# Two decoder blocks in one kernel: the forgetting term as a three-part bfloat16 product, and the turns of the probabilities at the end of a part

## The reference

```python
def forgetting_attention(q, k, v, log_f):       # 8 heads of 64
    c = jnp.cumsum(log_f, axis=1).transpose(0, 2, 1)
    ...
        s = jnp.einsum('bqhd,bkhd->bhqk', qb, k).astype(jnp.float32) * scale
        s = s + cq[..., None] - c[:, :, None, :]
        s = jnp.where((key_pos[None, :] <= qpos[:, None])[None, None], s, -jnp.inf)
        p = jax.nn.softmax(s, axis=-1).astype(v.dtype)
        return jnp.einsum('bhqk,bkhd->bqhd', p, v)
```

## Time and profile before

| | us |
|---|---|
| median of 3 runs (1918.96 to 1920.2) | 1919.72 |
| time of the profiled execution | 1919.35 |
| its span in the profile | 1917.2 |
| PE busy | 1901.4 |
| DVE busy | 1334.5 |
| ACT busy | 973.6 |

### The profile page before, as it was taken

The page is one execution under the profiler, slowest core; times in us unless marked ns, Lnnn a source line. Parts: engine busy times, 40 slices in busy tenths (PEclk is TensorE's granted clock), DMA queues, the critical chain, the costliest instruction groups (busy, mean ns, idle before and its releaser), DMA issues.

```text
span 1917.2 us, 26196 instructions
## 1 busy us (share of the span) xinstructions
PE 1901.4 (99%) x10969; PEld 1646.5 (86%) x10972; DVE 1334.5 (70%) x1461; ACT 973.6 (51%) x1227; POOL 151.7 (8%) x158
## 2 busy tenths in 40 slices
PE   9999999999999999999999999999999999999998
PEld 7888878888888888798888888888888888888887
DVE  7886677787678766868776554569865655569763
ACT  5444565544444445655444565445444665455442
POOL 0000422100000005211000110000000110000000
PEclk9999999999999999999999999999999999999999
DMA  7555533454555555324545443454555343445552
GB/s 285 208 183 185 194 111 111 154 198 170 184 198 194 175 199 183 121 95 161 191 179 186 151 175 132 175 177 166 196 182 185 130 163 138 166 176 182 181 181 105
DMA packets 47493, 327.31 MB, mean 171 GB/s; under 512 B 5520, under 2 KB 5520, under 8 KB 11536
## 3 DMA queue, kind: packets, MB, share of 16 engines
q1 hardware_dynamic: 46512, 323.25, 47.1%
q10 hardware_dynamic: 864, 2.39, 0.3%
HBM read 324.57 MB, written 1.05 MB: 170 GB/s over the span
## 4 chain that ended last, share of the span: by engine, by line
PE 95%; DVE 2%; ACT 1%; issue 1%; DMA 0%; POOL 0%; DVEq 0%; POOLq 0%; SPq 0%; ACTq 0%
PE ps L539 34%; PE ps L541 17%; PE ps L527 10%; PE ps L529 9%; PE ps L528 9%; PE ps L533 2%; PE ps L830 2%; PE ps L785 1%; PE ps L787 1%; PE ps L786 1%; PE ps L796 1%; PE ps L534 1%; PE ps L819 1%; PE ps L706 1%; PE ps L800 1%
## 5 line engine op out<-in xcount | busy, mean ns | idle before, releaser
L332 ACT CAST w_hi<-raw 128x2048 fp32r<-128x2048 f32 (+3 forms) x314 | 580.2, 1849 | 580.9 <-PE ps L541 351.8
L339 DVE TENSOR_TENSOR w_lo<-raw,w_hi 128x2048 fp32r<-128x2048 f32 (+3 forms) x314 | 699.1, 2228 | 246.2 <-ACT w_hi L332 243.4
L539 PE MATMUL ps<-x_hl,w_hi 128*128 128x512 f32 x1968 | 494.3, 393 | 0.0
L539 PEld LDWEIGHTS ps<-x_hl,w_hi 128*128 128x128 f32 x1968 | 353.8, 189 | 63.6
L541 PEld LDWEIGHTS ps<-x_hl,w_lo 128*128 128x128 f32 x1968 | 268.4, 190 | 19.3
L541 PE MATMUL ps<-x_hl,w_lo 128*128 128x256 f32 x1968 | 274.3, 282 | 0.0
L527 PE MATMUL ps<-w_hi,x_hl 128*128 128x512 f32 (+3 forms) x672 | 261.9, 390 | 0.0
L529 PE MATMUL ps<-w_hi,x_hl 128*128 128x512 f32 (+3 forms) x672 | 254.3, 378 | 0.0
L528 PE MATMUL ps<-w_lo,x_hl 128*128 128x512 f32 (+3 forms) x672 | 253.5, 377 | 0.0
L1789 DVE TENSOR_REDUCE ffn_tmp<-ps 128x512 f32<-128x1024 f32 x132 | 161.2, 1222 | 103.4 <-PE ps L541 102.6
L539 PE MATMUL ps<-hid_hl,w_hi 128*128 128x512 f32 x836 | 212.9, 394 | 0.0
(11 more groups left out here) (286 smaller groups left out, 2216.3 us busy)
## 6 DMA issues: line engine op xcount, KB each, us to landing
raw<-in_parts SPq DMA_DIRECT2D x278, 1024.0 KB, 4.8
raw<-in_parts SPq DMA_DIRECT2D x20, 768.0 KB, 4.1
raw<-in_parts SPq DMA_DIRECT2D x4, 928.0 KB, 4.5
raw<-in_parts SPq DMA_DIRECT2D x4, 864.0 KB, 4.7
raw<-in_parts SPq DMA_DIRECT2D x6, 512.0 KB, 3.7
raw<-in_parts SPq DMA_DIRECT2D x4, 576.0 KB, 3.9
const<-in_const ACTq DMA_DIRECT2D x1, 1098.0 KB, 5.2
h<-in_x_t SPq DMA_DIRECT2D x1, 1024.0 KB, 8.0
```

What stands on the lines that cost most here:

```text
L332: nc.scalar.copy(w_hi[:, i % RING, 0:n_of(i)], raw[:, i % RING, 0:n_of(i)]).then_inc(high_ready, 1)
L339: nc.vector.tensor_tensor(w_lo[:, s, 0:n], raw[:, s, 0:n], w_hi[:, s, 0:n].bitcast(F32), ALU.subtract).then_inc(low_ready, 1)
L539: nc.tensor.matmul(ps[:, bank, :], w_h(c), hl(c).rearrange("p x n -> p (x n)"), start=start and c == 0, stop=False, skip_group_check=True)
```

## The change

1. **Forgetting term.** `log_f` now holds the negated log gates three times, in columns 0 to 7, 32 to 39 and 64 to 71. The cumulated sums therefore stand three times in the bank. ACT copies the bank once to the bfloat16 tile `forget`; DVE subtracts this from the bank, writes the rest's bfloat16 over rows 32 to 63, and what is then left over rows 64 to 127. The products of line 800 now take `forget` and one column of the constant `head_rows`, which has ones in the three rows of the head, repeated to 128 columns; both are bfloat16. The part with c of the query is gone. `head_rows` is made once, in the first stage.
2. **Turns.** In both mixers PE's `batch_turn` of parts 10 to 14 and 16 to 19 moves from between the halves to the start of `after_part`, ahead of the scores. With it go two turns of q and k blocks (`qk_turn(7)` and `qk_turn(8)`).
3. **Copies.** In `mixer1` DVE's copy of a turned batch moves behind the `top_rounds` of its part, and in part 14 behind the gating. In part 12 it stands behind two rounds and ahead of `scale_heads`. In `mixer2` DVE's and ACT's lists are as before.

```diff
@@ constants
-    q_mul, q_add, k_mul, k_add = np.zeros((P, 8)), np.zeros((P, 8)), np.zeros((P, 1)), np.zeros((P, 1))
...
+    c["head_rows"] = (s % 32 == np.arange(8)[None, :]) * (s < 96) * 1.0
@@ batches1
-                        aug=[(q_aug[h0 + i][:, qt * P:(qt + 1) * P], k_aug[:, 0:nk]) for i in range(4)] if gate else None,
+                        aug=[(head_rows[:, h0 + i:h0 + i + 1].to_broadcast([P, P]), forget[:, 0:nk]) for i in range(4)] if gate else None,
@@ PE, mixer1
+                def after_part(m):
                     if m == 10:
                         pe.wait_ge(S["relu_ready"], 8)
                         turn_p(0)
...
-                def after_part(m):
...
-                        pe.wait_ge(S["aug_ready"], 9)
+                        pe.wait_ge(S["aug_ready"], 2)
                         qk_turn(6)
...
+                        pe.wait_ge(S["aug_ready"], 3)
                         scores(0)
@@ ACT, mixer1
-                    nc.scalar.activation(k_aug, cum, ACT.Identity, scale=cst("k_mul"), bias=cst("k_add")).then_inc(S["aug_ready"], 1)
-                    for hd in range(6):
-                        nc.scalar.activation(q_aug[hd], cum, ACT.Identity, scale=cst("q_mul")[:, hd:hd + 1],
-                                             bias=cst("q_add")[:, hd:hd + 1]).then_inc(S["aug_ready"], 1)
+                    nc.scalar.copy(forget[:, :], cum).then_inc(S["aug_ready"], 1)
@@ DVE, mixer1
+                def forget_terms():
+
+                    dve.wait_ge(S["aug_ready"], 1)
+                    nc.vector.tensor_tensor(forget_rest, ps[:, 1, 0:SEQ], forget[:, :], ALU.subtract).then_inc(S["aug_ready"], 1)
+                    dve.wait_ge(S["aug_ready"], 2)
+                    nc.vector.tensor_copy(forget[32:64, :], forget_rest[32:64, :])
+                    step(nc.vector.tensor_copy(forget[64:128, :], forget_rest[64:128, :]))
+                    nc.vector.tensor_tensor(forget[64:128, :], forget_rest[64:128, :], forget[64:128, :],
+                                            ALU.subtract).then_inc(S["aug_ready"], 1)
...
-                    if m >= 10:
-                        turned_p(m - 10)
                     if m == 12:
                         top_rounds(2)
+                        turned_p(2)
...
                     top_rounds({10: 4, 11: 4, 13: 2}.get(m, 0))
+                    if m >= 10 and m != 12:
+                        turned_p(m - 10)
...
-                        for hd in range(6, 8):
-                            nc.vector.tensor_scalar(q_aug[hd], ps[:, 1, 0:SEQ], cst("q_mul")[:, hd:hd + 1], cst("q_add")[:, hd:hd + 1],
-                                                    ALU.mult, ALU.add).then_inc(S["aug_ready"], 1)
+                        forget_terms()
```

More of the change, by code:

```diff
@@ L240, in build @@
         later_bf = sb("later_bf", [P, P], BF16)
+        head_rows = sb("head_rows", [P, 8], BF16)
+        forget = sb("forget", [P, SEQ], BF16)
         stat = sb("stat", [P, 212])
@@ L400, in build @@
         rope_a, rope_b = region(17824, (576,)), region(17824 + 576, (576,))
-        q_aug = ([proj[:, x // 2, C_Q + SEQ * (x % 2):C_Q + SEQ * (x % 2) + SEQ] for x in range(4)] +
-                 [proj[:, x // 2, I_Q + SEQ * (x % 2):I_Q + SEQ * (x % 2) + SEQ] for x in range(1, 4)] + [rows[:, 0, 0:SEQ]])
-        k_aug = proj[:, 0, I_Q:I_Q + SEQ]
+        forget_rest = proj[:, 0, I_Q:I_Q + SEQ]
         relu_r = ffn_tmp[:, 0:1024].rearrange("p (a b c) -> p a b c", a=2, b=2)
@@ L1187, in _ @@
                 if s == 1:
-                    pe.wait_ge(setup_done, 2)
+                    pe.wait_ge(setup_done, 3)
                 if tag == "mix":
@@ L1257, in ffn @@
                         nc.scalar.copy(later_bf[:, :], cst("later")).then_inc(setup_done, 1)
+                        act.wait_ge(tables_in, 16)
+                        nc.scalar.copy(head_rows[:, :], cst("head_rows")).then_inc(setup_done, 1)
                     if s == LAST and p in (7, 10, 13, 16):
@@ L2031, in after_part @@
                         dve.wait_ge(S["ln_ready"], 2)
-                        step(nc.vector.scalar_tensor_tensor(log_f[:, :, 0:8], z_f, 0.0, z_abs, ALU.min, ALU.subtract))
-                        nc.vector.tensor_scalar(log_f[:, :, 32:40], log_f[:, :, 0:8], -1.0, None, ALU.mult).then_inc(S["logf_ready"], 1)
+                        step(nc.vector.scalar_tensor_tensor(z_ln, z_f, 0.0, z_abs, ALU.min, ALU.subtract))
+                        for x in range(3):
+                            f = nc.vector.tensor_scalar(log_f[:, :, 32 * x:32 * x + 8], z_ln, -1.0, None, ALU.mult)
+                        f.then_inc(S["logf_ready"], 1)
                     if m == 7:
@@ L2038, in after_part @@
                         add_index(3)
-                        dve.wait_ge(S["aug_ready"], 7)
-                        for hd in range(6, 8):
-                            nc.vector.tensor_scalar(q_aug[hd], ps[:, 1, 0:SEQ], cst("q_mul")[:, hd:hd + 1], cst("q_add")[:, hd:hd + 1],
-                                                    ALU.mult, ALU.add).then_inc(S["aug_ready"], 1)
+                        forget_terms()
                     if m == 9:
```

## The result

| | before | with the change |
|---|---|---|
| median of 20 runs each, us | 1919.29 | 1922.57 |
| lowest and highest, us | 1918.85, 1920.23 | 1922.14, 1923.28 |
| profiled execution, us | 1919.35 | 1923.28 |
| its span, us | 1917.2 | 1921.2 |
| PE, DVE, ACT busy, us | 1901.4, 1334.5, 973.6 | 1899.3, 1338.1, 967.1 |

The changed kernel takes 1.0017 times as long as the kernel before, with a 95% interval of 1.001 to 1.0023. It is slower by 3.3 us, and the prediction had 1915.8 with a range of 1912.5 to 1919.5. The forecast missed by 6.8 us, and the time lies outside its range.

What follows compares the result with a forecast made beforehand. PE, busy 1901.4 of 1917.2 us, was taken as the bound. The first mixer's -5.4 and the second's +1.4 gave -4.0 us; with 0.37 to the median and 0.1 for signals, 1915.8 us, range 1912.5 to 1919.5.

Steps and rivals of the forecast that it cites:

- rival (B): Part 10, first mixer: the clock falls in PE's new wait; 1918.8 or 1926.9 us; chance short 0.14, long 0.05.
- short case: Low clock lasts as long as the wait in part 10: 1.5 us a layer, 1918.8 us; chance 0.14.
- long case: All of part 11 runs at the low clock: 5.56 us a layer, 1926.9 us; chance 0.05.
- the term: Forgetting products, first mixer: four at the mask's price, 0.77 us less for 128 keys, 1.39 less for 256.
- Rival (C): Forgetting products: the repeated column costs what float32 did; 3.1 us lost in all, 1918.9 us; chance 0.08.
- the wait of part 10: First mixer: PE stands still 3.1 us ahead of batch 0's values, for DVE's copy behind all six rounds.
- the 0.53 us of `qk_turn(6)`: Part 9, first mixer: the bank is free earlier, so this turn and what follows move 0.53 us earlier.
- The tie of part 11: First mixer: PE reaches the values at 280.1, with DVE's copy ready at 280.0.
- rival (D): A moved copy is later than the wait it removes; in part 12 too, 1916.8 us; chance with forecast 0.67.
- Part 13: First mixer: PE arrives at 297.9 and waits 1.8 us for the copy of batch 3; values start at 299.7.
- the second mixer: Openings save 0.3 us, a new wait in part 19 costs 1.0: 0.7 us more a layer, 1.4 in all.
- Rival (A): Copies come in time and PE keeps all: 6.2 us a layer in the first mixer, 1908.7 us; chance 0.06.

Runs made afterwards that it cites:

- half fill: Changed kernel with five bfloat16 products of 128x512, which nothing reads, in PE's wait in part 10 of the first mixer: 1919.85 us, ratio 0.9996.
- moved copy: Changed kernel with DVE's copy of batch 0 ahead of the four top rounds of part 10: 1918.28 us, ratio 0.9994.
- filled kernel: Changed kernel with twelve bfloat16 products of 128x512, which nothing reads, in PE's wait in part 10 of the first mixer: 1917.34 us, ratio 0.9991.
- turn of part 19: Changed kernel with the turn of the last batch of the second mixer back between the halves: 1920.31 us, ratio 1.0004.
- three copies ahead: Changed kernel with DVE's copies of batches 0, 1 and 3 ahead of the top rounds of parts 10, 11 and 13: 1910.74 us, ratio 0.9955.

## Why the prediction was wrong, point by point

**The step that failed** is the clock. The forecast's sum has no term for it, and the case that had one is rival (B): "for as long as the wait, it takes 1.5 us a layer, and the time is 1918.8". The prediction saw the danger and its place, and then priced it by the length of the wait. The lower level did not end with the wait; in the second layer it began only after it. It held for 6.8 us in the first layer and twice for 3.4 us in the second. The loss is 3.0 us in the first layer (9.48 against 6.48 from values to turn) and 3.1 in the second (1.6 and 1.5), between the short case's 1.5 and the long case's 5.56. Nor was the end of the trace, the only place of the earlier trace rows, able to say how long the low level lasts under work, since no work follows there. The two cases should have been one with a price from 1.5 to 5.56 and a large share of the chance, for the wait of about 3 us was the forecast's own, and the earlier trace rows showed that such a wait is enough. Instead 0.19 was given to it, "the wait may come out shorter than 2.8" was counted against it, and the range ended at 1919.5. What the prediction had named as a sign of being wrong, a granted clock under 1 in part 11, is what the trace shows. The time of 1922.57 is within the 0.2% that the prediction called no change (0.53), but measured well enough to be told from it.

The Trainium skill ("TensorE: Matmul & The Clock Gate", section "Why this matters for your kernels") warns of idle gaps of about the size of the wait in part 10 and has nothing against shorter ones. The trace agrees for the 2.82 us; the half fill and the moved copy show the clock falling behind idle times of 1.63 and 2.24 us as well, and there the measurement decides.

**A second wait that no case had priced.** In the second layer the wait of part 13, 1.07 us long, stands ahead of the second stretch of 3.4 us. The prediction put the clock only behind part 10. Whether this wait brings that fall is not shown. The same wait has no fall behind it in the first layer, nor in the second layer of the filled kernel's profiled execution; and in the traces that have the fall (the changed kernel, the half fill and the turn of part 19) another stands ahead of it in part 10 of the same layer.

**Right: the term.** 0.23 and 0.45 us against 0.22 and 0.44, so 0.76 and 1.38 us less instead of 0.77 and 1.39. Rival (C), a repeated column at the price of float32, did not happen.

**Right: the wait of part 10, and that the wait at the first turn goes.** PE waits 2.82 us by the profile, 2.98 from the mask's end (269.05 + 0.22) to the values, against 3.1. DVE's rounds and copy end 0.4 us after the time that was worked out (272.10 against 271.7).

**Wrong by a factor of two: the 0.53 us of `qk_turn(6)`.** The failed step is "eight records of 256 columns take 1.07 us ..., so these four 0.53". The four records of line 855 take 1.06 us (257.40 to 258.46), as long as eight of line 792. By the kernel's text line 855 forms two products on the same 64 rows of the array, and those of line 792 use both halves; the times say that the first come one after another and the second side by side. PE was busy, not waiting, and nothing was to be gained. That is 1.06 us of the sum, in two layers. The filled kernel shows a gain of 2.08 us in the first mixer; 2.7 less 0.53 is 2.17.

**The tie of part 11 and rival (D).** With the clock up, the values of part 11 follow the mask without a wait (280.80 to 281.02 in the filled kernel), and so do those of part 12: (D) did not happen there. It did once the copies were early: 0.29 us.

**Part 13: 1.8 expected, 1.07 measured.** In the filled kernel the copy ends at 300.24, 0.7 us after the predicted 299.55, and PE comes 1.4 later than the predicted 297.9: the head means came 0.6 us before their old time (286.04 against 286.66), not 1.3.

**Right: the second mixer.** The wait is 0.77 us instead of 1.0. Of the 0.3 us of openings little came. Parts 16 to 18 took 30.92 us without a split (1153.57 to 1184.49) and 31.01 with one (1151.36 to 1182.37), which is 0.09 less for three openings instead of 0.24. Eight transposes cost 0.79 us ahead of a half and 0.87 ahead of scores (1168.95 to 1169.82), and 0.96 ahead of those of the first mixer (281.73 to 282.69). The term "which I price at nothing" was not nothing. Together 0.80 us a layer against 0.7.

**Rival (A)** priced the change with the copies in time at 1908.7. With three copies ahead it is 1910.74; the 1.06 us of `qk_turn(6)`, 0.58 of the wait in part 12 and the openings are the rest. That PE's gain depends on the copies' place is what the prediction said; that the clock would turn the lost gain into a loss it didn't.

The sum with the terms corrected: -2.17 + 0.80 = -1.4 a layer, -2.7 in all, and +6.1 from the clock (3.0 + 1.6 + 1.5): 3.4 us slower, against 3.9 between the profiled executions and 3.3 between the medians.

## What to carry to other kernels

When an edit shortens the work between a producer and its reader, look at what that work hid; here a shorter term and a later copy were each harmless, and together made a wait of 2.8 us. Waits of TensorE of 1.6 us and more could bring the lower clock in these runs, so such a wait is to be priced at its own length and at the clock behind it, which stayed down for 3.4 or 6.8 us, longer than the wait itself. Before work is taken off the engine that sets the time, move up the small copies that it waits for.

## What the runs showed of the hardware that was not expected

- The lower clock outlasts the wait that it follows: in the changed kernel it held for 6.8 us in one place and 3.4 in two, and cost 3.0, 1.6 and 1.5 us. It can also begin after the wait has ended: 0.5 us and 1.8 us after, with PE at work. The idle times ahead of low clock were 2.82, 2.24, 1.63 and 1.07 us (for the last it is open whether it had a part in it). The same 1.63 and the same 2.23 were also followed by full clock in the other layer of the same execution, and 1.07 in the first layer of the changed kernel. What decides between the two wasn't tried and stays open.
- Filling a wait with products that nothing reads took 5.2 us off the time.
- A bfloat16 stationary operand that repeats one column costs as much as an ordinary one: 0.23 us for four of 128 columns, 0.45 for four of 256.
- Two float32 products of 64 rows and 256 columns on the same rows take 1.06 us; four, two on each half of the rows, take 1.07.
